# Second layer's query and key projections by head pairs, interleaved with stick-breaking attention, and memory products placed in the norm chain

## The reference, cut to what matters

```python
xn = rms_norm(x, p['attn_pre_g'])
proj = xn @ p['w_in']                       # layer 1: 768 q, 768 k, 768 v, 256 cross q
q, k, v, qc = jnp.split(proj, [SELF_W, 2 * SELF_W, 3 * SELF_W], axis=-1)
# stick-breaking, per head and block of 128 queries
z = jnp.einsum('bhqd,bhkd->bhqk', q_blk, kt) * scale
causal = s_idx[None, :] < t_idx[:, None]
log_1m = jnp.where(causal, jax.nn.log_sigmoid(-z), 0.0)
later = lax.cumsum(log_1m, axis=3, reverse=True) - log_1m
w = jnp.where(causal, jnp.exp(jax.nn.log_sigmoid(z) + later), 0.0)
out = jnp.einsum('bhqk,bhkd->bhqd', w, vt)
# both mixers
mem_n = rms_norm(mem, p['mem_g'])
cross_out = memory_cross_attention(qc, mem_n, p['w_mem_kv'])   # kv = mem_n @ w_mem_kv, softmax
mixed = jnp.concatenate([self_out, cross_out], axis=-1) @ p['w_out']
h = h + rms_norm(mixed, p['attn_post_g'])
```

## Time and profile before

| | us |
|---|---|
| median of 3 runs | 1591.87 |
| lowest, highest | 1591.09, 1593.0 |
| the profiled execution, device time | 1591.31 |
| its span in the trace | 1589.5 |
| PE, DVE, ACT, POOL busy in the span | 1480.7, 1114.4, 944.3, 101.7 |

### The profile page before, as it was taken

How to read it: one execution, slowest core, us unless ns; L and a number is a source line. 1 busy time by engine, 2 the same in 40 slices (tenths; PEclk the granted TensorE clock), 3 DMA queues, 4 the chain that set the end, 5 groups by cost and what they waited for, 6 DMA issues and landing times.

```text
span 1589.5 us, 18574 instructions
## 1 busy us (share of the span) xinstructions
PE 1480.7 (93%) x6691; PEld 1187.1 (75%) x6691; DVE 1114.4 (70%) x828; ACT 944.3 (59%) x796; POOL 101.7 (6%) x172
## 2 busy tenths in 40 slices
PE   5968899999898788999999999999999999999993
PEld 4544688888785547888888888888888888888882
DVE  2273554554320337889889889889889889889886
ACT  2042434343222825778778778778778778778773
POOL 3000100000100012101001001001001002001001
PEclk9977999999999888999999999999999999999997
DMA  8410764655334055999999999999999999999993
GB/s 279 143 43 5 273 205 167 206 170 205 106 106 159 1 197 174 399 382 370 395 370 371 393 371 368 394 367 372 394 364 375 388 375 371 388 379 366 390 376 140
DMA packets 175813, 448.88 MB, mean 282 GB/s; under 512 B 8800, under 2 KB 10912, under 8 KB 159648
## 3 DMA queue, kind: packets, MB, share of 16 engines
q1 hardware_dynamic: 171520, 433.65, 74.7%
q0 software_dynamic: 4256, 14.74, 2.4%
HBM read 442.04 MB, written 6.32 MB: 282 GB/s over the span
## 4 chain that ended last, share of the span: by engine, by line
PE 85%; DVE 5%; ACT 4%; issue 3%; DMA 1%; SPq 1%; POOL 0%; ACTq 0%; DVEq 0%; POOLq 0%
PE psum L528 23%; PE psum L530 22%; PE psum L529 22%; PE psum L397 7%; PE psum L408 4%; ACT w_hi L890 2%; PE psum L769 2%; PE psum L380 1%; DVE w_lo L1204 1%; PE psum L386 1%; PE psum L435 1%; DMA raw<-in_l_w_mem_kv 1%; DVE nmax L1155 1%; DVE reg_a L1172 0%; PE psum L801 0%
## 5 line engine op out<-in xcount | busy, mean ns | idle before, releaser
L1204 DVE TENSOR_TENSOR w_lo<-raw,w_hi 128x2048 fp32r<-128x2048 f32 x381 | 868.3, 2291 | 185.0 <-ACT w_hi L890 183.8
L890 ACT ACTIVATE w_hi<-raw 128x2048 fp32r<-128x2048 f32 x381 | 730.6, 1920 | 272.6 <-PE psum L530 272.5
L528 PE MATMUL psum<-w_hi,x_hi 128*128 128x512 f32 x1120 | 443.9, 396 | 11.7 <-DVE x_lo L1199 8.8
L530 PE MATMUL psum<-w_hi,x_lo 128*128 128x512 f32 x1120 | 437.6, 391 | 0.0
L529 PE MATMUL psum<-w_lo,x_hi 128*128 128x512 f32 x1120 | 437.0, 390 | 0.0
L528 PEld LDWEIGHTS psum<-w_hi,x_hi 128*128 128x128 f32 x1120 | 210.9, 188 | 57.3 <-DVE x_lo L1199 7.4
L530 PEld LDWEIGHTS psum<-w_hi,x_lo 128*128 128x128 f32 x1120 | 210.7, 188 | 45.0
L529 PEld LDWEIGHTS psum<-w_lo,x_hi 128*128 128x128 f32 x1120 | 211.1, 188 | 42.1
L528 PE MATMUL psum<-w_hi,h_hi 128*128 128x512 f32 x560 | 218.8, 391 | 0.0
L530 PE MATMUL psum<-w_hi,h_lo 128*128 128x512 f32 x560 | 217.9, 389 | 0.0
L529 PE MATMUL psum<-w_lo,h_hi 128*128 128x512 f32 x560 | 217.9, 389 | 0.0
(11 more groups left out here) (229 smaller groups left out, 892.9 us busy)
## 6 DMA issues: line engine op xcount, KB each, us to landing
raw<-in_l_w_gate SPq DMA_DIRECT2D x128, 1024.0 KB, 7.5
raw<-in_l_w_up SPq DMA_DIRECT2D x127, 1024.0 KB, 7.9
raw<-in_l_w_down SPq DMA_DIRECT2D x126, 1024.0 KB, 7.2
raw<-in_l_w_in SPq DMA_DIRECT2D x14, 1024.0 KB, 6.4
raw<-in_l_w_out SPq DMA_DIRECT2D x8, 1024.0 KB, 7.3
raw<-in_l_w_mem_kv SPq DMA_DIRECT2D x4, 1024.0 KB, 7.0
memb<-in_mem SPq DMA_DIRECT2D x2, 512.0 KB, 3.9
gains<-in_l_mem_g POOLq DMA_DIRECT2D x2, 512.0 KB, 7.5
```

The lines of the kernel that those rows point to most:

```text
L528: pe.matmul(out, x[0], w[0], start=first, stop=False, skip_group_check=True)
L530: return pe.matmul(out, x[1], w[0], start=False, stop=last, skip_group_check=True)
L890: act.activation(w_hi[:, m % CUT, :], raw[:, n % RAW, :], ACT.Copy).then_inc(hi_ok, 1)
L1204: dve.tensor_tensor(w_lo[:, m % CUT, :], raw[:, n % RAW, :], w_hi[:, m % CUT, :].bitcast(F32), ALU.subtract).then_inc(lo_ok, 1)
```

## The change

**Memory products.** PE transposes the memory tokens before the last `down` (both tiles), with bank 4 used for the first and the last of the four transposes; ACT and DVE drain them before the post-norm FPOST0 instead of inside the chain. `kmT` is computed at once after the last `down`, then tile 0 of `xn` is transposed, then the first half of `vm`, tile 1 of `xn`, and the second half.

The diff, cut to its core (removed code that only moved is left out in places):

```diff
+PAIRS = (4, 5, 0, 1, 2, 3)
+PAIR_COUNT = {p: n + 1 for n, p in enumerate(PAIRS)}
+PAIR_BEFORE = {p: PAIRS[n - 2] for n, p in enumerate(PAIRS) if n >= 2}
+MIX1 = (6, 4)
...
-        soft = reg_a[:, 0:1536].rearrange("p (u b c) -> p u b c", u=2, b=2)
-        stick = reg_b[:, 0:1536].rearrange("p (u b c) -> p u b c", u=2, b=2)
+        soft = memb[:, :, :].rearrange("p t d -> p (t d)")[:, 0:1536].rearrange("p (u b c) -> p u b c", u=2, b=2)
+        stick = xn[:, :, :].rearrange("p t d -> p (t d)")[:, 0:1536].rearrange("p (u b c) -> p u b c", u=2, b=2)
...
-        IN1 = [(i * 512, (i + 1) * 512) for i in (4, 0, 1, 2, 3)]
+        def head_cols(w, g):
+
+            w = w.rearrange("(k p) n -> p k n", p=P)
+            return [w[:, :, r * NH * HD + g * 256:r * NH * HD + (g + 1) * 256] for r in range(2)]
...
-        for lo, hi in IN1:
-            loads += cols(t["l1_w_in"], lo, hi)
+        loads += cols(t["l1_w_in"], 2048, 2560)
+        loads += head_cols(t["l1_w_in"], 2)
+        loads += cols(t["l1_w_in"], 1536, 2048)
+        loads += head_cols(t["l1_w_in"], 0)
+        loads += head_cols(t["l1_w_in"], 1)
...
             turn_hidden(NB - 1, 1)
+            turn(MEM1, "mem1T", (4, 5, 6, 4), src=memb)
             down(NB - 1, 0)
             down(NB - 1, 1)
...
-            turn(MEM1, "mem1T", (4, 5, 6, 7), src=memb)
             turned("mem1T")
-            memory_kv(1, memT, (4, 5))
-            turn(PRE1, "x1T", (0, 1, 2, 3))
+            w = Block()
+            begin(("kmT", 1), 4)
...
+            end(ins, ("kmT", 1))
+            turn(PRE1, "x1T", (0, 1, 2, 3), [0])
+            begin(("vm", 1), 5)
+            for tt in range(NT):
+                if tt == 1:
+                    turn(PRE1, "x1T", (0, 1, 2, 3), [1])
...
+            for u, layer, g, tt, q, k, keys, val, kt0 in UNITS1:
+                scores(u, layer, g, tt, q, k, keys)
+            head_cols_in("q", 2, 6)
+            head_cols_in("k", 2, 7)
+            for u, layer, g, tt, q, k, keys, val, kt0 in UNITS1:
+                turn_probs(u, MEM // P)
+            drained_all(("q", 2), ("k", 2))
+            stick_scores(4)
+            stick_scores(5)
...
+                rows(("v1a", tt), 6 + tt, xT, tt, w, 0, 512)
...
+                weigh(u, g, MEM // P, val, kt0, 4 + u % 2)
+            stick_sum(4)
+            stick_sum(5)
+            head_cols_in("q", 0, 6)
+            head_cols_in("k", 0, 7)
+            drained_all(("v1b", 0), ("v1b", 1))
+            stick_weigh(4, 4)
+            stick_weigh(5, 5)
+            drained_all(("q", 0), ("k", 0))
+            stick_scores(0)
+            stick_scores(1)
+            head_cols_in("q", 1, 6)
+            stick_sum(0)
+            stick_sum(1)
+            head_cols_in("k", 1, 7)
+            drained_all(("v1a", 0), ("v1a", 1))
+            stick_weigh(0, 4)
+            stick_weigh(1, 5)
+            drained_all(("q", 1), ("k", 1))
+            stick_scores(2)
+            stick_scores(3)
...
+            early, late = (4, 5, 6, 7, 0, 1), (2, 3)
+            wo = [Block(), Block()]
...
+            mix_part(0, early, False)
+            stick_sum(2)
+            stick_sum(3)
+            mix_part(1, early, False)
+            stick_weigh(2, 0)
+            stick_weigh(3, 1)
+            drained_all(("os", 2), ("os", 3))
+            mix_part(0, late, True)
+            mix_part(1, late, True)
...
-                turn(FPRE1, "f1T", (4, 5, 6, 7), [tt])
+                turn(FPRE1, "f1T", (2, 3, 6, 7), [tt])
```

More of the change, by code:

```diff
@@ L639, in _ @@
-            w = Block()
-            for tt in range(NT):
-                rows(("v1a", tt), tt, xT, tt, w, 0, 512)
-            w.done(("v1a", 1))
+            w = Block()
+            begin(("kmT", 1), 4)
+            for c in range(2):
+                for k in range(KD):
+                    ins = pe.matmul(bank(4, c * S, (c + 1) * S), w.at(k, c * P, (c + 1) * P), memT[:, k, :],
+                                    start=(k == 0), stop=(k == KD - 1))
+            end(ins, ("kmT", 1))
+            turn(PRE1, "x1T", (0, 1, 2, 3), [0])
@@ new lines, in _, with __init__, at, done @@
+            begin(("vm", 1), 5)
+            for tt in range(NT):
+                if tt == 1:
+                    turn(PRE1, "x1T", (0, 1, 2, 3), [1])
+                for k in range(KD):
+                    ins = pe.matmul(bank(5, tt * 256, (tt + 1) * 256), memT[:, k, tt * P:(tt + 1) * P],
+                                    w.at(k, 256, 512), start=(k == 0), stop=(k == KD - 1))
+            end(ins, ("vm", 1))
+            w.done(("vm", 1))
+            turned("x1T")
+            class HeadBlock:
+                def __init__(self, label):
+                    self.n, self.label = n_raw[0], label
+                    pe.wait_ge(raw_full[self.n % RAW], 16 * (self.n // RAW + 1))
+                    n_raw[0] += 1
+                def at(self, k, lo, hi):
+                    return raw_at(self.n, KD, 256)[:, k, lo:hi]
+                def done(self):
+                    free_after[self.n] = bk.full(self.label)
@@ new lines, in _, with mix_part @@
+            stick_scores(3)
+            early, late = (4, 5, 6, 7, 0, 1), (2, 3)
+            wo = [Block(), Block()]
+            def mix_part(tt, ks, last):
+                for hf in range(2):
+                    label = ("mix", 1, tt, hf)
+                    b = MIX1[tt] + hf
+                    if not last:
+                        begin(label, b)
+                    for k in ks:
+                        ins = pe.matmul(bank(b), mixT[:, k, tt * P:(tt + 1) * P], wo[hf].at(k, 0, FB),
+                                        start=(k == early[0]), stop=(k == late[-1]))
+                    if last:
+                        end(ins, label)
+                        if tt == NT - 1:
+                            wo[hf].done(label)
```

209 lines of the change are left out of this document (110 added, 99 removed).

## The result

The changed kernel takes 1571.2 us (median of 4 executions, 1569.9 to 1571.8), the kernel before on the same chip 1591.5. The ratio is 0.9876, with a 95% interval of 0.9864 to 0.9889. The forecast was 1572.5 us, in a range from 1567 to 1581. The profiled execution has a span of 1570.0 us and a device time of 1571.8.

The account below looks back on a forecast made before the run. TensorE was taken to bound the expert stretch, so gains ahead of it count fully. Memory stage 3.8 plus stick-breaking 21.6 less norm chain 6.0 gives 19.4 us off the median 1591.87: 1572.5 us, range 1567 to 1581.

Parts of the forecast that it names:

- What bounds the kernel: Expert stretch: TensorE busy 951.87 of 968 us sets its length, so earlier work moves the end one for one.
- Rival (d): Experts: DMA engines, not TensorE, set the pace and the gain is given back, 1591 us; chance 0.03.
- Memory stage: Memory projections and transposes: waits of 2.93 and 1.05 us go, less 0.2; 3.8 us gained.
- tile 1's pre-norm: Memory stage: has 0.8 us of slack, costed at nothing; if late it costs about 1 us.
- the term for the fourth transpose: Memory stage: the fourth transpose shares a bank with the first, costing 0.2 us.
- Stick-breaking: Six pairs and their waits, interleaved with projections: 21.5 + 1.5 + 0.5 = 23.5 us in place of 45.1; 21.6 gained.
- The wait before the second sum: Stick-breaking, pairs 0 and 1: softplus usable after 12.15 us, 10.6 us of work between; a wait of 1.5 us.
- Rival (a): Stick-breaking: small steps do not pack, every hand-over costs a wait like 0.49 or 1.05 us; about 1579 us, chance 0.17.
- rival (c): First stick scores to output projection's end: TensorE's clock falls to half over 93 us; 1619 us, chance 0.04.
- Norm chain: Norms after M, the output projection's end: tile 1's addition ends at M + 10.9, was M + 5.0; 6.0 us lost.
- Loads: New 1 MB head loads land in 8.6 us, nothing waits; four expert pieces issued some 25 us earlier.
- The sum: Whole kernel: 3.8 + 21.6 - 6.0 = 19.4 us gained.

Follow-up runs that it names:

- run without cover: Changed kernel with the 12 output-projection products between scores and sums of pairs 2 and 3 moved behind these sums: 1581.4 us, ratio 0.9937.
- the run with the early cuts: Changed kernel with ScalarE's cuts of expert pieces 0 and 1 ahead of its copies of the last two head outputs, VectorE's following: 1570.3 us, ratio 0.9870.
- the filler: Changed kernel with tile 0 complete first, cuts of pieces 0 and 1 early, and 78 unused identity products in TensorE's waits before the gather: 1567.5 us, ratio 0.9860.

## Why the prediction came out right

**What bounds the kernel** held: the expert stretch kept its length (981.3 and 981.2 us), so what was won ahead of it reached the end whole in these two traces. The second fall of the clock, which lengthens this stretch by 1.2 to 2.1 us in other traces, is in neither of them; the prediction had no term for it. Rival (d), the gain given back there, did not happen: the DMA share is 0.99 as before and TensorE is busy 951.90 of 967.20 us.

**Memory stage, 3.8 forecast, 4.3 measured,** three times (28.74, 28.75 and 28.75 us against 33.06 and 33.03). Both waits went, and the uncertain term, tile 1's pre-norm, cost nothing. Of the 0.5 us more, 0.2 are the term for the fourth transpose, which shares a bank: no wait shows there (the transposes start at 400.51, the next product at 402.26). The rest is that a set of transposes takes 1.75 us from start to start where 1.91 had been added from an entry's length, tail and all.

**Stick-breaking, 21.6 forecast, 22.6 measured.** The three kinds of term all held. The work of six pairs is 20.3 us, not 21.5: the scores take 0.80 a pair, a weighing 0.75, a sum 1.8 (1.76 to 1.89); the sum of 1.95 came from a stretch of the earlier trace rows with a wait before it and a weighing behind it. The wait before the second sum is 1.35 where 1.5 was worked out from 12.15 - 10.6. The 12.15 was a misreading: no wait stands at 521.56 in the earlier trace rows, so that is when TensorE came and not when the softplus was usable. VectorE had finished it at 521.22, 11.8 us after the scores started, as its timeline before shows:

```profile
520.80 0.42 DVE L1344 TENSOR_TENSOR reg_a<-reg_a,clamp 128x256 f32<-128x256 f32 x1
```

The traces with a wait there show 11.9. The last copy is 0.56 for 0.5. The output projection, in four parts, is 0.2 us longer than in one. Rival (a), a wait at each hand-over, and rival (c), the clock, are answered by the windows: busy 36.00 of 36.00 us from 461 to 497, the two waits named behind it, and clock 1.00 throughout. The price of rival (c) was wrong in its last step. The first sum at half clock takes 3.4 us in place of 1.8 in the run without cover, so 93 us of work would have cost up to another 93 by this estimate, and not 46. TensorE's work in this stretch was tested without its cover only at pairs 2 and 3; for the other pairs the trace stands alone.

**Norm chain, -6.0 forecast, -6.0 measured** up to the experts, 5.8 of it at tile 1's addition, and step by step: VectorE busy until M - 0.9 (M - 0.7), scale of tile 0 at M - 0.1 (M + 0.1), next pre-norm scale at M + 4.8 (M + 5.0), scale of tile 1 at M + 8.0, addition's end at M + 10.8 (M + 10.9). That VectorE's cut shuts GpSimd's small operation out was drawn from one row and from the Trainium skill, page "SBUF — State Buffer", section "Who interferes with whom". The traces here agree: the run with the early cuts shows 0.18 us in place of 1.25 once the cut is out of the way. What the prediction had no term for is the gather's share of half clock: 5.42 us before, 5.68 after, and up to 6.8 in the variants. That it came out nearly equal in these two traces is luck, as two traces of one kernel differ by 1.5 us there.

**Loads.** The estimate of 8.6 us for a 1 MB load with rows of 1 KB was too high: the six such loads land in 5.0 to 8.3 us, four of them within 5.9, the wide ones around them in 5.1 to 7.4. Nothing waited for them, so nothing hung on it. The expert pieces were not all issued 25 us earlier either: the first two are issued 1 us earlier and 10 us later than before (507.1 and 519.1 us for 508.2 and 508.6), the next two 20 us earlier. None was waited for.

**The sum** came within 0.1 us of 19.4 in the two profiled executions partly by luck: memory and stick-breaking brought 1.5 us more than forecast, and the profiled execution after happened to start 1.5 us late. By the stretches alone the change is worth 21.0 us, and the changed kernel's second measurement, 22.5 us below before, lies on that side.

## What to carry to other kernels

Where an engine waits in a chain over several engines, cost the new order by two things only: its own work in that chain, and for each wait the length of the chain less the work that now lies in between; here that gave a wait of 1.5 us where 1.35 came. When products are moved so that all tiles finish together, the overlap of the first tile's epilogue is lost; finishing one tile early keeps the gain in the middle and the overlap at the end (5.1 us at the last addition here, 4.2 at the first expert product, for a change of order). Look for large VectorE operations beside small GpSimd ones on a critical chain. And take a second trace of the same kernel before an edit of 1 us is judged: here two of them differ by 3.2 us behind the same instruction.

## What was not expected of the hardware

- TensorE's grant rises at a different time in each execution, measured from M, inside the gather or near its end. The same 32 matmul instructions take 3.74 us at full clock, 5.24 us in one trace of a kernel and 6.79 in another of the same. In six of fourteen traces it falls again for some 3 us at the start of the experts.
- A fall of the clock ahead of a second wait was free as far as that wait: in the run without cover the first sum took 3.4 us and not 1.8, and M still moved by 8.5 us where 8.8 were forecast.
- A 128x128 product of the identity in float32 takes 0.23 us of TensorE at full clock, where a transpose of the same shape takes 0.11 (8 of them from 555.27 to 556.17, where the filler starts). In the trace the product is two matmul instructions (68 for 34 products) and the transpose is one.
- The start of the program varies by up to 6 us over executions (396.0 to 402.1 us at the last hidden transposes), more than most of the edits tried here are worth.
